# A two-layer hybrid trunk on one core: another order of the work between attention and the first expert

## The reference

```python
def moe_swiglu(h, w_router, w_gate, w_up, w_down):
    logits = (h @ w_router).astype(jnp.float32)
    top_val, top_idx = lax.top_k(logits, TOP_K)          # 2 of 8
    top_w = jax.nn.softmax(top_val, axis=-1)
    gates = jnp.sum(jax.nn.one_hot(top_idx, N_EXPERTS, dtype=jnp.float32) * top_w[..., None], axis=-2)
    out = jnp.zeros_like(h)
    for e in range(N_EXPERTS):
        out = out + gates[..., e:e + 1] * swiglu(h, w_gate[e], w_up[e], w_down[e])
    return out
# around it: h = rms_norm(x, norm_g[1, 2]);  x = x + rms_norm(out, norm_g[1, 3])
```

## Time and profile before

| | us |
|---|---|
| median of 3 runs | 1231.81 |
| the three runs | 1231.81, 1235.57, 1231.67 |
| the profiled execution, its own time | 1235.62 |
| its span | 1233.8 |
| PE busy in it | 1201.3 (97%) |
| DVE busy | 686.5 (56%) |
| ACT busy | 539.6 (44%) |
| POOL busy | 144.0 (12%) |

### The profile page before, as it was taken

One profiled execution on the slowest core, in us unless ns is written; L12 is line 12 of the kernel. 1 busy time (PEld: TensorE's weight loads), 2 busy tenths in 40 slices (PEclk: granted clock), 3 DMA queues, 4 the chain that ended last, 5 costly groups with the idle time before them and its releaser, 6 DMA issues.

```text
span 1233.8 us, 15258 instructions
## 1 busy us (share of the span) xinstructions
PE 1201.3 (97%) x5922; PEld 845.5 (69%) x5922; DVE 686.5 (56%) x761; ACT 539.6 (44%) x525; POOL 144.0 (12%) x141
## 2 busy tenths in 40 slices
PE   9999999989989999999999999999999999999996
PEld 8888887778878888434788833578883357887332
DVE  4844455646577988101888710288861038895102
ACT  3743334445546776002677500267750036774001
POOL 0000000000025460100006020000602000050200
PEclk9999999999989999999999999999999999999999
DMA  9955553653376999899999999999999999999994
GB/s 296 361 184 192 180 195 116 198 185 109 109 279 244 370 364 366 334 420 421 422 422 421 419 393 419 423 422 423 419 408 392 420 422 423 422 419 387 397 421 189
DMA packets 128279, 413.52 MB, mean 335 GB/s; under 512 B 10753, under 2 KB 30209, under 8 KB 113794
## 3 DMA queue, kind: packets, MB, share of 16 engines
q1 hardware_dynamic: 127394, 409.28, 85.2%
q0 software_dynamic: 816, 3.28, 0.8%
HBM read 411.48 MB, written 1.05 MB: 334 GB/s over the span
## 4 chain that ended last, share of the span: by engine, by line
PE 85%; DVE 7%; DMA 6%; ACT 1%; SPq 1%; issue 1%; DVEq 0%; ACTq 0%
PE bank L1480 19%; PE bank L1482 19%; PE bank L1481 19%; PE bank L1862 14%; DMA raw<-in_moe_w_gate 5%; PE bank L1875 4%; DVE raw_lo L972 3%; PE bank L1814 1%; PE bank L1942 1%; PE bank L1896 1%; PE bank L1487 1%; SPq L582 1%; DMA head_row<-in_heads 1%; PE bank L1738 1%; DVE y L1391 1%
## 5 line engine op out<-in xcount | busy, mean ns | idle before, releaser
L972 DVE TENSOR_TENSOR raw_lo<-raw,w_hi 128x2048 fp32r<-128x2048 f32 x148 | 337.9, 2303 | 72.1 <-ACT w_hi L641 71.6
L641 ACT ACTIVATE w_hi<-raw 128x2048 fp32r<-128x2048 f32 x149 | 284.5, 1917 | 122.1 <-PE bank L1482 75.7
L1480 PE MATMUL bank<-w_hi,h_hi 128*128 128x512 f32 x568 | 226.4, 399 | 9.8 <-DVE h_lo L1335 5.3
L1481 PE MATMUL bank<-raw_lo,h_hi 128*128 128x512 f32 x576 | 225.0, 391 | 0.0
L1482 PE MATMUL bank<-w_hi,h_lo 128*128 128x512 f32 x568 | 222.6, 392 | 0.0
L1862 PE MATMUL bank<-raw,h_b 128*64 128x512 f32 (+1 forms) x768 | 143.1, 523 | 0.0
L1480 PEld LDWEIGHTS bank<-w_hi,h_hi 128*128 128x128 f32 x568 | 107.1, 189 | 40.7 <-issue 11.5
L1481 PEld LDWEIGHTS bank<-raw_lo,h_hi 128*128 128x128 f32 x576 | 108.7, 189 | 21.9
L1482 PEld LDWEIGHTS bank<-w_hi,h_lo 128*128 128x128 f32 x568 | 106.9, 188 | 23.2
L972 DVE TENSOR_TENSOR raw_extra_lo<-raw_extra,w_hi 128x2048 fp32r<-128x2048 f32 x48 | 112.9, 2372 | 14.6 <-ACT w_hi L641 14.4
L1862 PEld LDWEIGHTS bank<-raw,h_b 128*64 128x64 f32 x768 | 53.6, 137 | 82.5 <-issue 73.9
(11 more groups left out here) (320 smaller groups left out, 1624.4 us busy)
## 6 DMA issues: line engine op xcount, KB each, us to landing
raw<-in_moe_w_gate SPq DMA_DIRECT2D x96, 1024.0 KB, 13.6
raw<-in_moe_w_up SPq DMA_DIRECT2D x80, 1024.0 KB, 14.4
raw<-in_moe_w_down SPq DMA_DIRECT2D x64, 1024.0 KB, 13.9
raw_extra<-in_moe_w_down SPq DMA_DIRECT2D x48, 1024.0 KB, 16.1
raw_extra<-in_moe_w_up SPq DMA_DIRECT2D x32, 1024.0 KB, 12.5
raw_extra<-in_moe_w_gate SPq DMA_DIRECT2D x16, 1024.0 KB, 10.4
raw<-in_ffn_w_gate SPq DMA_DIRECT2D x11, 1024.0 KB, 5.3
raw<-in_ffn_w_up SPq DMA_DIRECT2D x11, 1024.0 KB, 5.0
```

The source lines that it names most:

```text
L641: nc.scalar.activation(to, raw_slot(source), ACT.Copy).then_inc(hi_ready, 1)
L972: nc.vector.tensor_tensor(lo_slot(source), raw_slot(source), high.bitcast(f32), ALU.subtract).then_inc(lo_ready, 1)
L1480: mm(out, a_hi, b_hi, start=first, stop=False)
L1481: mm(out, a_hi, b_lo, start=False, stop=False)
```

## The change

It moves and reshapes the work of the joint. On POOL the gain product keeps only the first half of block 0, and the last gain's transfer and both memsets come behind `he_lo_done` 2. DVE takes the rest of the gain product, finds the best experts of block 0 before it and of block 1 behind it, and compares both blocks in one go. The first unit is split whole behind `sel` and not in two halves. The ranking of the experts is cut in two (`shares`, `shares_rest`), which with `gate_shares` go between splits of the first pair. The router's and rank products read their 8 columns 16 times over and so write 128. `keep_warm` counts change.

```diff
-WARM = (8, 6, 0, 8, 0, 4, 6)
+WARM = (8, 6, 4, 4, 3, 5, 6)
...
-            def top_two(tb):
+            def top_found(tb):
                 ve.wait_ge(lg_psum, tb + 1)
                 link(nc.vector.tensor_copy(lg[:, tb, :], bank[4 + tb][:, 0:E]))
                 link(nc.vector.max(top[:, tb, :], lg[:, tb, :]))
                 link(nc.vector.max_index(topi[:, tb, :], top[:, tb, :], lg[:, tb, :]))
-                link(nc.vector.tensor_copy(topf[:, tb, :], topi[:, tb, 0:2]))
...
-            top_two(0)
-            lo_half(MOE_U0, 0)
-            top_two(1)
+            top_found(0)
+            gain_landed(6)
+            nc.vector.tensor_tensor(xn[:, 1, :], x[:, 1, :], gain[:, 0, :], ALU.mult).then_inc(xn_done, 1)
+            nc.vector.tensor_tensor(xn[:, 0, HALF:D], x[:, 0, HALF:D], gain[:, 0, HALF:D], ALU.mult).then_inc(xn_done, 1)
+            top_found(1)
+            link(nc.vector.tensor_copy(topf[:, :, :], topi[:, :, 0:2]))
+            link(nc.vector.tensor_tensor(m12[:, :, :, :], iota8[:, None, None, :].to_broadcast([P, TB, 2, E]),
+                                         topf[:, :, :, None].to_broadcast([P, TB, 2, E]), ALU.is_equal))
+            nc.vector.tensor_tensor(mboth[:, :, :], m12[:, :, 0, :], m12[:, :, 1, :], ALU.add).then_inc(m_done, 1)
             root(6, 0, TB)
...
-            lo_half(MOE_U0, 1)
+            lo(MOE_U0)
+            nc.vector.tensor_copy(rank[:, :, :], rank_ps).then_inc(rank_copied, 1)
+            ve.wait_ge(rank_psum, 2)
+            nc.vector.tensor_copy(count, bank[4][:, 0:E]).then_inc(rank_copied, 1)
...
+                if is_pair(p, 0):
+                    shares()
+                    lo_to(AHEAD)
+                    shares_rest()
+                    lo_to(AHEAD + 2)
+                    gate_shares()
                 lo_to(last_up(0) + 2)
...
             def residual_transposed(tb):
                 for i in range(2):
+                    if tb == 1:
+                        keep_warm(WARM[2 + 2 * i])
...
+            def repeated(columns):
+                return columns[:, None, :].to_broadcast([P, P // E, E])
...
-                    step = mm(bank[4 + tb][:, 0:E], x_t[:, k, tb * P:(tb + 1) * P], wr_g[:, k, :], start=(k == 0),
-                              stop=(k == KB - 1))
+                    step = mm(bank[4 + tb][:, 0:P], x_t[:, k, tb * P:(tb + 1) * P], repeated(wr_g[:, k, :]),
+                              start=(k == 0), stop=(k == KB - 1))
...
-            mm(bank[5][:, 0:E], before, mboth[:, 0, :], start=True, stop=True)
+            mm(bank[5][:, 0:P], before, both[0], start=True, stop=True)
...
-            pe.wait_ge(xn_done, 4)
+            pe.wait_ge(xn_done, 5)
...
-            free = {3: (x_done, 2), 4: (x_done, 2), 5: (x_done, 4), 6: (xn_done, 2), 7: (x_done, 6)}
+            free = {3: (x_done, 2), 4: (x_done, 2), 5: (x_done, 4), 6: (xn_done, 2), 7: (he_lo_done, 2)}
...
-                    for tb in range(TB):
-                        po.wait_ge(x_done, 5 + tb)
-                        if tb == 1:
-                            po.wait_ge(x_front, 1)
-                        nc.gpsimd.tensor_tensor(xn[:, tb, :], x[:, tb, :], gain[:, 0, :], ALU.mult).then_inc(xn_done, 1)
+                    po.wait_ge(x_done, 5)
+                    nc.gpsimd.tensor_tensor(xn[:, 0, 0:HALF], x[:, 0, 0:HALF], gain[:, 0, 0:HALF],
+                                            ALU.mult).then_inc(xn_done, 1)
...
-            po.wait_ge(unit_used, MOE_U0)
             for tb in range(TB):
                 nc.gpsimd.memset(y[:, tb, :], 0.0).then_inc(acc_done, 1)
```

More of the change, by code:

```diff
@@ L1304, in top_two @@
                 link(nc.vector.max_index(topi[:, tb, :], top[:, tb, :], lg[:, tb, :]))
-                link(nc.vector.tensor_copy(topf[:, tb, :], topi[:, tb, 0:2]))
[L1306 to L1310, removed]
-            top_two(0)
-            lo_half(MOE_U0, 0)
-            top_two(1)
+            top_found(0)
[7 more added lines that the diff above has]
+            nc.vector.tensor_tensor(mboth[:, :, :], m12[:, :, 0, :], m12[:, :, 1, :], ALU.add).then_inc(m_done, 1)
             root(6, 0, TB)
-            ve.wait_ge(m_done, 2)
+            ve.wait_ge(m_done, 1)
             link(nc.vector.tensor_scalar(away[:, :, :], mboth[:, :, 0:1], float(-2 * T), float(2 * T),
@@ L1320, in _ @@
             ve.wait_ge(rank_psum, 1)
[L1321 to L1322 removed]
+            rank_ps = bank[5][:, 0:TB * P].rearrange("p (b n) -> p b n", n=P)[:, :, 0:E]
+            count = ctab[:, 11, :]
             link(nc.vector.tensor_tensor(pos0[:, :, :], rank_ps[:, :, 0:1], away[:, :, :], ALU.add))
@@ L1342, in _ @@
             lo(MOE_U0 + 2)
[L1344 to L1355, removed]
@@ new lines, in shares @@
+            def shares():
+                ve.wait_ge(rank_copied, 2)
+                link(nc.vector.scalar_tensor_tensor(key, count, float(E), tie, ALU.mult, ALU.add))
+                link(nc.vector.tensor_tensor(ahead[:, :, :], key[:, None, :].to_broadcast([P, E, E]),
+                                             key[:, :, None].to_broadcast([P, E, E]), ALU.is_gt))
+                link(nc.vector.reduce_sum(place, ahead[:, :, :], AX.X))
+                nc.vector.tensor_scalar(base, place, float(CAP + CAP_B), None, ALU.mult)
+                link(nc.vector.tensor_scalar(small, place, float(PAIRS), None, ALU.is_ge))
@@ new lines, in shares_rest @@
+            def shares_rest():
+                link(nc.vector.tensor_scalar(cap, small, float(CAP_B - CAP), float(CAP), ALU.mult, ALU.add))
+                link(nc.vector.scalar_tensor_tensor(base, small, float(CAP - PAIRS * (CAP + CAP_B)), base,
+                                                    ALU.mult, ALU.add))
+                link(nc.vector.tensor_tensor(big, count, cap, ALU.is_gt))
+                link(nc.vector.tensor_tensor_scan(incl, big, big, 0.0, ALU.add, ALU.bypass))
+                nc.vector.tensor_scalar(rtab_i[:, 0:1], incl[0:1, E - 1:E], float(PAIRS), None,
+                                        ALU.add).then_inc(pairs_done, 1)
@@ L1798, in _ @@
             keep_warm(WARM[5])
-            pe.wait_ge(m_done, 2)
+            pe.wait_ge(m_done, 1)
             ones, before = consts[:, C_ONES:C_ONES + P], consts[:, C_TRIS:C_TRIS + P]
-            mm(bank[5][:, 0:E], before, mboth[:, 0, :], start=True, stop=True)
-            mm(bank[5][:, E:2 * E], ones, mboth[:, 0, :], start=True, stop=False)
-            mm(bank[5][:, E:2 * E], before, mboth[:, 1, :], start=False, stop=True).then_inc(rank_psum, 1)
-            mm(bank[4][:, 0:E], ones, mboth[:, 0, :], start=True, stop=False)
-            mm(bank[4][:, 0:E], ones, mboth[:, 1, :], start=False, stop=True).then_inc(rank_psum, 1)
+            both = [repeated(mboth[:, tb, :]) for tb in range(TB)]
+            mm(bank[5][:, 0:P], before, both[0], start=True, stop=True)
+            mm(bank[5][:, P:2 * P], ones, both[0], start=True, stop=False)
+            mm(bank[5][:, P:2 * P], before, both[1], start=False, stop=True).then_inc(rank_psum, 1)
+            mm(bank[4][:, 0:P], ones, both[0], start=True, stop=False)
+            mm(bank[4][:, 0:P], ones, both[1], start=False, stop=True).then_inc(rank_psum, 1)
             def gather(ready, slots):
```

21 lines of the change are left out of this document (6 added, 15 removed).

## The result

| | before | after |
|---|---|---|
| median, same chip | 1232.7 (6 runs, 1229.74 to 1235.57) | 1225.57 (6 runs, 1220.06 to 1227.02) |
| ratio, with its 95% interval | | 0.9928 [0.9905, 0.995] |
| the profiled execution | 1235.62 | 1226.45 |
| its span | 1233.8 | 1224.6 |
| first expert product, from the span's start | 375.83 | 365.32 |

The medians lie 7.1 us apart, the ratio says 8.9 (6.2 to 11.7), and the forecast was 7.4. The kernel is faster, by more than the 0.3% that a measurement of it can tell from no change, and 1225.57 stands 1.2 beside the forecast of 1224.4.

A forecast was written before the change was run, and what follows sets the result against it. The joint was taken as bound by a chain from engine to engine ending at PE's first expert product. 7.2 + 0.5 - 0.3 = 7.4 us off the median 1231.81 gives 1224.4; range 1222.0 to 1229.8.

The forecast's parts named there:

- Block 1's sums: Joint, DVE: one-column sum L995 falls from 1.00 to 0.16, so x_front and x_done 6 come 0.84 earlier.
- Wider products: Router and rank products on PE: 128 columns take 1.95 for 16 MATMULs like 8 columns; repeated columns cost nothing.
- PE up to the second router product: Joint, PE: with seven added keep_warm products, block 1's router product ends at 360.6 where it was 362.58.
- DVE: Joint: gain products hidden by the router product; mboth at 362.0 instead of 366.13, sel at 364.95, 4.1 earlier.
- PE up to the experts: Joint, PE: gather at 365.0 instead of 371.88 (6.9); first expert product at 368.6, 7.2 earlier.
- The first units: First pair's splits: fourth split before the ranking, which follows in two pieces; no idle time, 0.5 gained with the restart.
- The memsets: POOL's memsets (1.86) beside the first units' splits: idle PE between nothing and 1.4, taken as 0.3.
- Handed on: Rounds after the joint: loads move with PE, the whole shift is handed on and nothing is given back.
- The 3.8 between levels: Whole kernel: profiled execution 3.8 above the median; the last pair's start explains 1.6, the rest couldn't be placed.
- that of the clock: Rival, joint: clock falls all the same; 2.2 saved, 1229.6, a shorter fall up to 5; chance 0.13.
- The slower case: Rival: first up product waits for POOL's late memsets, held 14.6 in all, starting 8.0 late: 1232.4; chance 0.03.
- the late splits: Rival, first units: splits come late beside the memsets; 6.3 saved, 1225.5; chance 0.08.

The follow-up runs named there:

- the order alone: The changed kernel with 8-column products and the old keep_warm counts, DVE and POOL as changed: 1228.74, ratio 0.9964.
- two halves: Changed kernel with PE as before (1228.74, ratio 0.9964); changed kernel with DVE and POOL as before, wide products and new keep_warm kept (1231.79, ratio 0.9996).
- the head filled: The changed kernel with 12 keep_warm products before the wait for v_done of the first head: 1224.18, ratio 0.9923.

## Why the prediction was right

- **Block 1's sums** (0.16) and `x_front`: as predicted, and the kernel with both gain products on POOL shows the term by itself: the sum is 0.82 longer there, and the first expert product 0.64 later.
- **Wider products cost next to nothing**: 2.01 for 16 where I had 1.95. I had them in the sum at nothing, and what the clock does had no term in it either; in truth the width carries a large part of the gain. Narrow again, the products cost 3.1 of the 7.26. So the forecast of the full clock was right, and its reason, that the holes are filled and the products wide, only in its second half.
- **PE up to the second router product**: 2.08 earlier, predicted 1.98. The fillers that I counted with are not what kept the clock; without them it stayed too, and the product ended 0.23 earlier still.
- **DVE**: `mboth` and `sel` 4.3 earlier for 4.1 predicted, the gain products hidden with 0.41 to spare.
- **PE up to the experts**: gather 6.95 earlier (6.9), first expert product 7.26 (**7.2**).
- **The first units**: the fourth split's idle time was worth 0.75 (measured by the ranking put back, 0.74), where I had taken 0.5. My own count had it nearly right: a fifth unit at 379.6 is 8.0 before 387.56, and so 0.8 beyond the 7.2.
- **The memsets**: 0, where I had taken 0.3 of a range of 0 to 1.4. The Trainium skill's page that the prediction names beside this term (SBUF — State Buffer, "Who interferes with whom") gave 0, and the trace agrees: a split of 2.28 beside memsets of 1.87. These two terms are the only ones that were mis-sized, and they add up: 8.0 for 7.4.
- **Handed on**: the shift isn't lost. From the fifth unit to the second pair's gather pass 188.6 us and 188.5 before, and to its first expert product 198.1 and 197.5: PE waits 2.10 for `h_lo` there where it waited 1.53. This wait runs from 1.39 to 2.39 in the nine traces with DVE's new order and no fillers in it, so the 0.6 belongs to the run as far as they show. Counted from J the second pair starts 7.4 earlier, above the 7 that I had set. "Later pairs as long as before" held only up to the falls: the second pair took 213.5 here and 212.4 before, the third 212.6 and 212.3, the last with the end 224.1 in both.
- **The 3.8 between levels** was the thing I couldn't place. The traces offer pieces for it: the clock at the start (up to 4.05), at the wait of 250 us (1.5) and at the starts of pairs (1.1 in the second, 1.6 in the last). Together that is nearly as much as the change itself brings. That they made these 3.8 isn't shown, as only one execution of the kernel before has a trace. And two levels was the wrong picture: 34 runs of it on one chip lie between 1227.49 and 1239.49, with no gap over 1.5 between neighbours.
- **Luck**: that the medians lie 7.1 apart, so near to 7.4, is partly chance, since the joint gave 8.0 and each median moves with the falls outside it.

Of the **rivals**, that of the clock came true in the two changed kernels with narrow products: with the change's fillers 4.2 were saved at the first expert product (I had up to 5 for a shorter fall), and the order alone saved 2.23, which meets my 2.2 partly by chance, since it has other fillers than I had counted. But the reason I gave for it, the Trainium skill's rule (TensorE: Matmul & The Clock Gate, "PE-mode transpose") that transposes don't count as activity, would have let the clock fall with the fillers taken out, and there it stayed at 1.00 over eight transposes and a hole of 0.73. The trace doesn't bear the rule out for this place. It doesn't disprove it either, since the wide products around may be enough by themselves. The slower case and the late splits had nothing to them: POOL's memsets took 1.87 beside a split, and PE ran on without idle time.

## What to carry to other kernels

Where a chain of short steps passes between PE and DVE, making one engine's part faster is worth little alone: here two halves of 2.2 and 2.4 gave 7.3 together, so try such parts together before dropping either of them. Read the granted clock beside PE's busy share: small products whose columns can be repeated for nothing should be made wide, and an instruction of POOL belongs beside DVE instructions that it doesn't hold. Before comparing two profiles, cut both at the same instruction and look where else the clock fell; and put fillers only where PE would stand still, since at the start of this kernel they stood in its way.

## What the runs showed of the hardware

- 16 MATMULs of 8 columns and 16 of 128 take nearly the same time at full clock (1.95 and 2.01 to 2.05), but the clock fell behind the narrow ones with PE's row full (1.00 of 1.00 us from 354), and held behind the wide ones with PE busy for 1.11 of 2.00 us.
- Waits of about 2 us at a pair's start may or may not bring the clock down. 2.10 and 2.11 did (the changed kernel), 1.82 did (its fourth pair with the head filled); 1.89 and 2.06 did not (the order alone), nor did 2.26 (the third pair with the products back to 8 columns). The length of the wait doesn't decide it; what does is left open.
- The same instructions at the program's start end up to 4.2 apart from one run to the next (the next part's first product at 24.05 to 28.21 over thirteen traces).
- Beside POOL's two memsets (1.86) and the issue of a transfer in front of them (0.60), a DVE pair of `tensor_scalar` of 8 columns took 2.0 us longer, and a two-input product of 1024 columns no longer than without them (1.23).
